# A two-layer diffusion trunk on one core: the first three projections in two halves, and two waits and a branch moved

## What is computed

```python
for l in range(DEPTH):                                  # DEPTH = 2, for context and for latent tokens
    sh1, sc1, gt1, sh2, sc2, gt2 = _modulation(cond, w_mod[l], b_mod[l])   # silu(cond) @ w_mod + b_mod
    h = _rmsnorm(x, g_mix[l]) * (1 + sc1) + sh1
    (aq, ak, av), (mq, mk, mv, ig, lf), og = _project(h, w_in[l], ...)     # one matrix, 1024 x 2832
    att = _block_attention(aq, k_all, v_all)
    h_ml, fin_f, fin_b = _mlstm_bidir(mq, mk, mv, ig, lf, init_f, init_b)
    x = x + gt1 * _mixer_out(att, h_ml, og, g_mh[l], w_out[l])
    h = _rmsnorm(x, g_ffn[l]) * (1 + sc2) + sh2
    x = x + gt2 * _moe(h, w_router, b_router, w_e_gate[l], w_e_up[l], w_e_down[l])
```

## Time and profile before

| | |
|---|---|
| median of 3 runs | 801.32 us (800.31 to 803.5) |
| the profiled execution | 802.08 us, span 800.3 us |
| TensorE busy | 761.7 us (95%), 4685 instructions |
| VectorE, ScalarE, GpSimd busy | 329.3, 158.1, 56.6 us |
| HBM read | 286.31 MB, on average 361 GB/s over the span |
| mean granted TensorE clock | 0.993 of full |
| chain of waits, by engine | PE 77%, DMA 15%, DVE 3%, issue 2%, SPq 2% |
| costliest lines | L1099 151.6 + 46.2 us, L764 125.3, L1129 92.1 + 35.4, L1014 59.3 |

### The profile page before, as it was taken

One profiled execution on the slowest core, in us unless ns is written; L12 is line 12 of the kernel. 1 busy time (PEld: TensorE's weight loads), 2 busy tenths in 40 slices (PEclk: granted clock), 3 DMA queues, 4 the chain that ended last, 5 costly groups with the idle time before them and its releaser, 6 DMA issues.

```text
span 800.3 us, 10926 instructions
## 1 busy us (share of the span) xinstructions
PE 761.7 (95%) x4685; PEld 403.4 (50%) x4691; DVE 329.3 (41%) x534; ACT 158.1 (20%) x355; POOL 56.6 (7%) x69
## 2 busy tenths in 40 slices
PE   3899999989999999999889999999999999999997
PEld 2364547866534434444234646688753443444423
DVE  0379467513422331223218965782332223212323
ACT  2202125401412002020003111261131201202001
POOL 0040060100200000000000003300010000000000
PEclk9999999989999999999999999999999999999999
DMA  8999809997999999999999880579969999999993
GB/s 351 397 381 379 352 7 387 405 373 315 425 422 425 423 421 424 427 418 424 422 403 410 311 317 0 190 292 394 379 245 405 428 425 420 424 427 418 424 422 154
DMA packets 49857, 289.41 MB, mean 362 GB/s; under 512 B 3400, under 2 KB 5760, under 8 KB 23696
## 3 DMA queue, kind: packets, MB, share of 16 engines
q1 hardware_dynamic: 48080, 285.30, 87.7%
q0 software_dynamic: 1488, 3.31, 1.2%
q10 hardware_dynamic: 240, 0.08, 0.0%
HBM read 286.31 MB, written 2.37 MB: 361 GB/s over the span
## 4 chain that ended last, share of the span: by engine, by line
PE 77%; DMA 15%; DVE 3%; issue 2%; SPq 2%; ACT 1%; POOL 0%; ACTq 0%; DVEq 0%
PE ps L1099 22%; PE ps L764 14%; PE ps L1129 12%; DMA ring<-in_w_e_up 9%; PE ps L1014 6%; PE ps L1083 4%; DMA ring<-in_w_in 3%; PE ps L639 3%; PE ps L1144 2%; PE ps L778 2%; SPq L544 1%; DMA ring<-in_x_sample 1%; DMA out_new_state_n<-nst 1%; PE ps L1111 1%; PE ps L892 1%
## 5 line engine op out<-in xcount | busy, mean ns | idle before, releaser
L1099 PE MATMUL ps<-ring,xe 128*64 128x512 f32 x688 | 151.6, 594 | 3.7 <-DMA ring<-in_w_e_up 3.7
L764 PE MATMUL ps<-ring,hT 128*128 128x512 f32 (+1 forms) x320 | 125.3, 551 | 2.6 <-DMA ring<-in_w_in 2.6
L1099 PEld LDWEIGHTS ps<-ring,xe 128*64 128x64 f32 x688 | 48.6, 137 | 104.7 <-issue 100.1
L764 PEld LDWEIGHTS ps<-ring,hT 128*128 128x128 f32 x320 | 60.2, 190 | 64.3 <-issue 58.2
L1129 PE MATMUL ps<-ring,ex 128*32 128x512 f32 x736 | 92.1, 594 | 0.2 <-issue 0.2
L1991 DVE COPY ye<-ps 64x512 f32<-64x512 f32 (+1 forms) x28 | 19.3, 689 | 162.8 <-PE ps L1129 162.6
L1014 PE MATMUL ps<-hT,ring 128*128 128x256 f32 x256 | 59.3, 391 | 0.0
L1975 DVE RECIPROCAL ex<-ex 128x512 f32<-128x512 f32 x16 | 53.6, 3353 | 0.6
L1014 PEld LDWEIGHTS ps<-hT,ring 128*128 128x128 f32 x256 | 49.5, 196 | 8.1 <-issue 1.0
L1129 PEld LDWEIGHTS ps<-ring,ex 128*32 128x32 f32 x736 | 26.0, 110 | 52.2 <-issue 49.5
L1973 DVE TENSOR_SCALAR ex<-ex 128x512 f32<-128x512 f32 x16 | 6.8, 427 | 109.4 <-ACT ex L1525 109.4
(11 more groups left out here) (270 smaller groups left out, 809.4 us busy)
## 6 DMA issues: line engine op xcount, KB each, us to landing
ring<-in_w_mod SPq DMA_DIRECT2D x24, 2048.0 KB, 19.5
ring<-in_w_e_up SPq DMA_DIRECT2D x23, 2048.0 KB, 19.0
ring<-in_w_e_gate SPq DMA_DIRECT2D x20, 2048.0 KB, 22.7
ring<-in_w_e_down SPq DMA_DIRECT2D x19, 2048.0 KB, 22.2
ring<-in_w_in SPq DMA_DIRECT2D x10, 2048.0 KB, 23.3
beside<-in_w_e_gate SPq DMA_DIRECT2D x8, 2048.0 KB, 25.3
beside<-in_w_e_down SPq DMA_DIRECT2D x7, 2048.0 KB, 19.5
beside<-in_w_e_up SPq DMA_DIRECT2D x5, 2048.0 KB, 17.7
```

The source lines that it names most:

```text
L764: mm = pe.matmul(bank[:, 0:width], hT[:, k, b * P:(b + 1) * P], w[:, k, :], start=(k == 0), stop=(k == KD - 1))
L1099: mm = pe.matmul(bank[PLACES * j:PLACES * j + PLACES, :], xe[:, k, c:c + PLACES], w[:, j, i, :], start=(k == 0), stop=(k == KD - 1))
```

## The change

Four things.

1. **Section 0 of layer 0 is loaded and computed by features.** It becomes two sections, -1 and 0. Section -1 covers the first 512 features of shift and of scale (two blocks of all eight k and 512 columns, runs of 2 KB), section 0 the other 512. `feature_rows` computes 32 matmuls of 128 columns per block where `section_rows` had 8 of 512; `feature_columns` builds shift and `amp` for half of the features. hT is then made for k 0 to 3 from section -1 and for k 4 to 7 from section 0. The samples and constants are loaded ahead of all of w_mod.
2. **mk, mq and mv of layer 0 are loaded and computed in two contraction halves.** The order of loads is: section -1 (two blocks), the first halves of mk, mq, mv (1 MB each, each half signals a semaphore `front_in`), section 0 (two blocks), the second halves, the four blocks of section 1, aq and the rest. TensorE runs the three first halves with section 0's rows and columns between them, then the three second halves. mq's banks are cleared by a product with zeros first. mv moves to banks 4 and 5, the gates to 6 and 7. The sums of section 1 in layer 0 are taken in turns (0, 1), (2), (3) instead of (0, 1, 2), (3), (): the last turn stands between the first gaps and akv's copies. On TensorE the rows of biases are turned after x, and a few warming products stand ahead of x.
3. **`state_out` is no longer awaited by ScalarE and VectorE in the middle of the layer.** VectorE waits for it at the head of the next layer; ScalarE's wait there was there before. GpSimd's and SyncE's waits stay.
4. **In layer 0 the last scatter stands ahead of the branch**, in layer 1 behind it as before.

The core of the diff:

```diff
+SECTION_CHUNKS[0, -1], SECTION_CHUNKS[0, 0] = (0, 8), (4, 8)
+HALVED = ("mk", "mq", "mv")
-SUM_TURNS = (((0, 1, 2), (3,), ()), ((0, 1, 2), (3,), ()))
+SUM_TURNS = (((0, 1), (2,), (3,)), ((0, 1, 2), (3,), ()))
...
+    for i in range(section_slots(0, -1)):
+        put(("mod", 0, -1, i))
+    for g in HALVED:
+        put((g, 0))
     for i in range(section_slots(0, 0)):
         put(("mod", 0, 0, i))
     for l in range(DEPTH):
         for g in PROJ:
-            put((g, l))
+            if l > 0 or g not in HALVED:
+                put((g, l))
             for i in BETWEEN.get(g, ()):
                 put(("mod", l, 1, i))
...
-            load_section(0, 0, 0)
             sp.dma_start(cst[:, 0:P], t["constants"][:, 0:P]).then_inc(const_in, 16)
             for b, name in enumerate(("x_prompt", "x_sample")):
                 sp.dma_start(xtok[:, b, :], t[name][0]).then_inc(x_in, 16)
-            load_section(0, 0, 1, 2, 3)
...
+            load_features(-1)
+            for g, landed in zip(HALVED, front_in):
+                load_rows(g, slice(0, KD // 2), landed)
+            load_features(0)
+            for g in HALVED:
+                load_rows(g, slice(KD // 2, KD), slot_landed[weights[g, 0][0]])
...
+            def feature_rows(s, *which):
+                bank = begin(("modrow", 0, s)) if 0 in which else ps[banks["modrow", 0, s][0]]
+                for v in which:
+                    w = landed(("mod", 0, s, v)).rearrange("p (k n) -> p k n", k=KD)
+                    for k in range(KD):
+                        for g in range(4):
+                            mm = pe.matmul(bank[32 * g:32 * g + 32, v * P:(v + 1) * P], cT[:, NB * k:NB * k + 32],
+                                           w[:, k, g * P:(g + 1) * P], start=(k == 0), stop=(k == KD - 1))
...
+                    for b in range(NB):
+                        norm_parts(l, b)
                     pe.wait_ge(cond_silu, 1)
-                    section_rows(0, 0, 0)
+                    feature_rows(-1, 0)
+                    for b in range(NB):
+                        norm_total(l, b)
+                    feature_rows(-1, 1)
+                    warm((("mk", 0), l), 3)
+                    section_columns(0, -1)
...
+                if l == 0:
+                    front, back = range(0, KD // 2), range(KD // 2, KD)
+                    project("mk", fresh=True, ks=front)
+                    project_turned("mq", range(NB), front)
+                    feature_rows(0, 0, 1)
+                    project("mv", (0,), ks=front)
+                    section_columns(0, 0)
+                    project("mv", (1,), ks=front)
+                    project("mk", fresh=True, ks=back)
+                    project_turned("mq", (0,), back)
+                    gates()
+                    project_turned("mq", (1,), back)
+                    gate_rows()
+                    project("mv", ks=back)
...
+                if l + 1 < DEPTH:
+                    scatter_pair(PAIRS - 1, 0, KD)
                 with pe.If(limit[0] > SLOTS):
...
-                scatter_pair(PAIRS - 1, 0, KD)
+                if l + 1 == DEPTH:
+                    scatter_pair(PAIRS - 1, 0, KD)
...
-                act.wait_ge(state_out, 16 * STATE_OUTS * (l + 1))
                 squares_mid(l)
                 root_mid(l)
...
+                if l > 0:
+                    dve.wait_ge(state_out, 16 * STATE_OUTS * l)
                 normalise(l)
...
-                dve.wait_ge(mod_ready, 2 * l + 2)
-                dve.wait_ge(state_out, 16 * STATE_OUTS * (l + 1))
+                dve.wait_ge(mod_ready, 2 * l + 3)
```

More of the change, by code:

```diff
@@ L148, in bank_plan @@
         put(("x", r), r)
-    put(("modrow", 0, 0), 7)
-    put(("modcol", 0, 0), 7)
+    for s in (-1, 0):
+        put(("modrow", 0, s), 7)
+        put(("modcol", 0, s), 7)
     for l in range(DEPTH):
@@ L721, in _ @@
                 done(("x", r), mm)
+            pe.wait_ge(rows_in, 16 * ROW_LOADS * DEPTH)
+            for l in range(DEPTH):
+                bank = begin(("rows", l))
+                done(("rows", l), pe.transpose(bank[:, 0:ROWS_L], rowsin[:, l, :], ident[0:ROWS_L, 0:ROWS_L]))
             def section_sums(l, s):
```

142 lines of the change are left out of this document (94 added, 48 removed).

## The result

| | before | changed |
|---|---|---|
| median | 802.26 us (800.31 to 803.5, 6 runs) | 807.22 us (804.72 to 809.63, 6 runs) |
| ratio to before | 1 | 1.0058, 95% interval 1.0043 to 1.0073 |
| profiled execution, span | 802.08, 800.3 us | 804.86, 803.0 us |
| mean granted TensorE clock | 0.993 | 0.988 |

The change makes the kernel slower by 0.6%. The forecast was 799.3 us with a range of 795.0 to 805.5; the measured time lies above both, and it moved up where a small gain was forecast. The profiled execution lies 2.8 us above that of before, the medians 5.0.

What follows compares the result with a forecast made beforehand. Load queue and TensorE, both nearly full, bound it in turn; the queue sets layer 0's end. Profiled 802.08 + 3.9 (late aq) - 4.7 (queue hole) - 1.2 (branch) = 800.1, median 0.76 lower: 799.3 us, range 795.0 to 805.5.

Steps and rivals of the forecast that it cites:

- Front: the start of the projections: Head of layer 0: mk, the first projection, starts at 23.4 instead of 33.57, between 22.5 and 25.
- Front: the work behind it: TensorE from mk to mv's end: 43.9 us plus 4.5 added work, mv ending at 71.8 against 78.2, lead 6.4.
- Where the lead goes: Wait ahead of aq: aq starts at 79.9, 1.7 us later than before, after 8 us idle, plus 2.2 slow clock.
- the slot walk: Seven-slot load ring followed block by block: aq takes mv's slot, so it can be asked for only at 71.8.
- d: Delay of layer 0 from aq on: 3.9 us, bounds 0.5 and 7.
- VectorE and GpSimd: Front: rotary chain ends at 122.5 against 123.2, hidden by 0.7; gate loads land at 58.2, gates reached at 59.3.
- the slower rival: Front: gates wait for GpSimd's late loads, delaying mv and aq; at 7.3 us late the total is 805.5; chance 0.15.
- the rival in which the lead survives: Front: aq does not wait for mv's slot, delay -6.4, total change -12.3, so 789 us; chance 0.07.
- The state wait: Middle of layer 0: its 6.0 us cost to TensorE goes; the second queue hole closes, worth 4.7 us.
- The branch: End of layer 0: scatter ahead of the branch brings the first norm part earlier, 1.2 us gained, bounds 0 and 3.5.
- The sum: Whole kernel: profiled 802.08 + 3.9 - 4.7 - 1.2 = 800.1, median 0.76 below, so 799.3 us.
- the hole: Second gap in the load queue, in 185 to 195 of layer 0: closes, 4.7 us gained.

Runs made afterwards that it cites:

- e10: Changed kernel with the moved state waits and the moved scatter taken back, so the new front alone: 804.43 us, ratio 1.0034.
- e1: Changed kernel with aq loaded first behind the second feature half, in the first feature block's slot, section 1 following: 801.99 us, ratio 1.0.
- e2: Changed kernel with full-width zero products where TensorE waits, 38 ahead of aq and 13 around the last norm totals: 799.88 us, ratio 0.9973.
- e15: e1 with 51 small products of zeros at the start: 796.52 us, ratio 0.992.
- e12: e1 with most of VectorE's sums over section 1's third and fourth blocks left out, so part of the work missing: single run, 792.79 us.
- e3: Kernel before with only the state waits of ScalarE and VectorE moved out of the middle of the layer: 797.82 us, ratio 0.9949.
- e4: Kernel before with only layer 0's last scatter moved ahead of the branch: 798.32 us, ratio 0.9956.
- e9: Kernel before with 32 small products of zeros at the very start, where TensorE waits for data: 800.08 us, ratio 0.9975.
- e16: e15 with all work kept and VectorE's section 1 sums in turns of one block, one and two: 800.44 us, ratio 0.9969.

## Why the prediction was wrong

**Front: the start of the projections** was the first step that failed: 23.4 predicted, 26.8 measured, and 22.5 to 25 as bounds. The norms were ready early enough (their last total is at 17.02, where 19.1 was predicted), and the second feature block was last, not the norms by 1.1: its products start at 19.91 where 19.2 was predicted, +0.7. They took 3.64 us and not 1.9, +1.7. The price of the new form, which the prediction had only assumed, was right: 1.93 at full clock in the same kernel, with four times the instructions. The half clock in that stretch was not in the sum; the prediction weighed the clock only where TensorE idles for 8 us. The columns and hT then took 3.25 us instead of 2.3, +0.9. Together 3.4. In e10, where the second block's products ran at full clock (1.95 us), mk started at 24.18. In the ten profiles with this front it starts between 24.11 and 26.80, in none at 23.4 and in three inside the bounds, and in each of them the rows of at least one of the two blocks took 3.0 to 3.6 us. So the profiled run of the changed kernel had the worst case of this step, but the step was too short in all.

**Front: the work behind it** held: from mk's start to mv's end 48.3 us, predicted 48.4. **Where the lead goes** held as well: the wait is 8.49 us (8.1 predicted), released by the load, and e1 shows by its absence that the slot walk causes it. The slow clock behind it cost 15.80 - 13.9 = 1.9 (2.2 predicted, and e2 gives it back). So d, by which the section's columns are late (126.01 instead of 118.64), is 7.4 and not 3.9, and outside its upper bound of 7.

**VectorE and GpSimd** cost TensorE nothing in the changed kernel, but not for the reasons given. The gates had more room than thought: the second load of their weights, issued at 50.08, landed after 6.5 us at 56.6, and L853 started at 62.33 without a wait, so the slower rival did not occur. VectorE was late: its scans stood 6.93 us for `b_router`, which the prediction did not look at, and its rotary chain ended at 128.88, 2.2 us behind the section's columns, where 0.7 ahead was predicted. TensorE did not wait for either. That VectorE would be the bound as soon as aq comes early was not seen. With that, the rival in which the lead survives, 789 us, needed more than a free slot for aq: in e1 and e15 the columns come only 2.4 and 3.4 us earlier than in the changed kernel, and only e12, with the sums cut short, shows them 5.8 us ahead of the kernel before.

**The state wait** held in kind and size: no wait at `sdot`, hole closed, 4.46 us in e3 for 4.7 predicted. In the changed kernel the down projection ends at 414.85 against 412.56, 2.3 later; d - 4.7 would give 2.7.

**The branch** was the second step that failed. The gain of 1.2 us rested on the thought that the stall belongs to the branch. What stands there depends on the branch's place in the instruction stream. The edit gives 3.9 us in the old kernel's stream (e4), where a shift by 64 instructions alone shortens the same stretch as much (e9), and in the new stream it brings a stall that was not there without it (e10 has none). The rule of the Trainium skill that the prediction cites (Runtime: NRT & Kernel Launch, section Instruction fetch mechanics), by which TensorE pays for the jump behind the scatter too, was nearer to the changed kernel: the term would be 0, and from the down projection's end to mk are 11.7 us before and 11.8 after. The kernels without a stall show that it does not hold for every place of the branch. The row that layer 1 has no stall was in hand, and it said that the stall isn't a fixed price of the jump.

**The sum.** With the measured sizes, 802.08 + 7.4 - 5.1 (the hole, as the down projection shows it) + 0.1 (the branch) + some 0.3 in layer 1 gives the profiled 804.86. Of the miss in the profile, 804.86 - 800.1 = 4.8, d makes 3.5 and the branch 1.3; the hole gave 0.4 more, and layer 1 took 0.3. Then the prediction set the median 0.8 under the profiled execution, as before; here it lies 2.4 over it, which is another 3.1 us of the whole miss of 7.9. That step took one execution for typical, and its own base of three runs, 801.32, lay 0.9 under the median of six, 802.26.

## What to carry to other kernels

Before a stall named "issue" behind a jump is given to the code around it, shift the stream by a few dozen cheap instructions in an idle place: here 32 or 51 products of 0.03 us each removed 3.5 us. Two kernels whose jump stands at different places in the stream can differ by such a term of some 4 us, either way, whatever else was changed. A reordered load list is to be followed slot by slot to the first block behind it, and then once more with that wait taken out, for the engine that is late next. When parts of a change can be separated, run them apart: the state waits and the scatter were worth 1.0% together, about half of it through the place of the branch; the front took that back, and the stall, at its new place in the stream, is about the 0.6% of the result.

## What the runs showed of the hardware

- A jump can cost TensorE 2.7 to 3.6 us without a releaser in the profile (eight profiles), or nothing that is seen (eight others). In each of the eight stalls a single 16.4 KB packet of the instruction queue q8 moves, on the same 16 DMA engines as the loads, which move 383 to 412 GB/s there. Whether the stall would be shorter with idle DMA engines no run shows.
- The granted clock also fell without long idling ahead of it. In e4 and e9 the clock in 480 to 485 us is 0.66, with TensorE busy for all of these 5 us and for 4.59 of the 5 before; akv and mo take 22.59 us instead of 20.91. e1 and e16 show the like up to 5 us later (0.74 in 485 to 490, 0.76 in 480 to 485). The two windows and the row of e4:

```profile
475.00:480.00 5.00, 4.59 (x30) 2.85 (x28) 0.77 (x4) 0.60 (x1) 0.00 (x0) 1.00 0.00 0
480.00:485.00 5.00, 5.00 (x18) 3.96 (x16) 1.61 (x7) 1.06 (x1) 0.00 (x0) 0.66 0.00 0
```

```profile
480.17 22.59 PE L764 MATMUL ps<-ring,hT 128*128 128x256 f32 x64
```

  The kernel before and the changed one do the same work there at full clock, and the kernel before shows the same 4.59 us in 480 to 485, ahead of akv. What sets it off in four of the profiles is open.
